# Differential attention on one Trainium2 core: two softmax maps of a head merged before the transpose instead of after the values product

## The chip, the core and the metric

The kernel runs on one core of one Trainium2 chip. The metric is the device time of one execution in microseconds. A core has five engines that run on their own and wait for each other by semaphores: TensorE (PE in the rows, with its weight loads as PEld), VectorE (DVE), ScalarE (ACT), GpSimd (POOL) and SyncE (SP, which here only starts the weight transfers). Each engine executes its own instructions strictly in the order in which the program gives them.

## What is computed

Two stacked models of two layers each act on 256 tokens of width 1024. The program has twelve stages: feed-forward, mixer, feed-forward, four times over. The change touches the last mixer alone, the stage `dil_diff` of the eleventh place, in which four heads of dilated attention and four heads of differential attention are computed. The differential part of the reference:

```python
def one_block(args):
    i, qa, qb = args
    ...
    s1 = jnp.where(causal, jnp.einsum('bqhd,bkhd->bhqk', qa, k1)..., -jnp.inf)
    s2 = jnp.where(causal, jnp.einsum('bqhd,bkhd->bhqk', qb, k2)..., -jnp.inf)
    attn = jax.nn.softmax(s1, axis=-1) - lam * jax.nn.softmax(s2, axis=-1)
    return jnp.einsum('bhqk,bkhe->bqhe', attn.astype(v.dtype), v)
```

So each head has two causal 256x256 maps. Their difference, with the weight `lam`, multiplies the head's values. After that each head's output is normalised, put beside the dilated heads and multiplied by the output weights.

## The kernel before

**Weights.** All weights come in pieces of 128x2048 floats through three slots. SP loads a piece, ACT copies it to a rounded high part `w_hi` (`split_hi`, line L460), DVE forms the low part `w_lo` as the difference (`split_lo`, L933), and PE multiplies with three matmuls per product (L1504 to L1506), 48 of 512 columns for a piece. ACT and DVE work two pieces ahead: at the start of their program for piece p both take piece p + 2 (`ahead`).

**The stage dil_diff** has 16 pieces. Pieces 0 to 11 project the tokens to dq, dk, dv, cq, ck and cv, two pieces for each; pieces 12 to 15 are the product with the output weights. A piece has two token tiles (tt 0 and 1). After each tile of the pieces 5 to 11, PE's program has a hook, `with_tile`, that does a little attention work between the big matmuls. It counts steps: step = 2 (p - 6) + tt + 1, so step 0 lies in piece 5, steps 1 and 2 in piece 6, 3 and 4 in piece 7 and so on. ACT and DVE have the same steps in their programs, behind the weight work of that piece.

**Maps.** The eight maps of the differential heads are numbered g0 to g0 + 7 (head h has maps 2h and 2h + 1), the four of the dilated heads follow. One map takes this route, and the maps follow each other one step apart:

- `scores` on PE (L1711), into bank 4 or 5;
- `soft` on DVE: scale and mask (L1371), then two maxima (L1374, L1375);
- `exp_map` on ACT: two exponentials with their sums (L572, four rows in the trace), in place;
- `turn_probs` on PE: three 128x128 transposes into bank 6 (L1719), two steps behind the scores;
- `take_probs` on ACT: bank 6 to SBUF (L580);
- `values` on PE: three fp32 matmuls into bank 7 (L1730, L1732, L1733), three steps behind the scores.

When both maps of head h are through `values`, DVE's `take_pair` (L1254 to L1261) inverts the sums, multiplies the second by -lam, and scales and adds the two 128x128 results of each token tile: six instructions. `square_head` on ACT (L811), `head_mean_square` on DVE (L1277), a power on POOL (L339) and `norm_head` on DVE (L1283) follow. The probabilities of a map lie in one of two buffers (map number modulo 2), so `soft` of map g waits for the transposes of map g - 2.

**On POOL,** `rotate_cq` runs four elementwise instructions on SBUF (L355, L356, L358, L360) as soon as ACT has taken cq in its program for piece 7.

**Order on the engines.** There is no scheduler; the order is written out. ACT's program for a piece of the map steps, which also takes the projected chunk in odd pieces (L564), is

```python
ahead(n0 + p)
for step in steps_of(p, 6, 1):
    if 2 <= step < 10:
        take_probs(g0 + step - 2)
    if step < 8:
        exp_map(g0 + step, step)
    if step in (5, 7, 9):
        square_head((step - 5) // 2)
```

and DVE's is `ahead`, then for each step `soft`, and in even steps from 4 `take_pair`. At piece 10 DVE also rotates ck (L1360 to L1363).

Of the kernel before, what the change touches and what calls it, by code (L numbers as in the profile page):

```python
# [71 lines left out]
def build(nc, program, t):  # L72
# [16 lines left out]
    with ExitStack() as ctx:  # L89
# [61 lines left out]
        merged_ready = sem("branches_merged")  # L151
        id_in = sem("ident_in")
# [107 lines left out]
        def psum3(b, k):  # L260
# [8 lines left out]
                       cqt=1024, ckt=1024, qa=1024, qb=1024, dkt=1024, diff=1024, sq=1024, prod=256,  # L269
# [18 lines left out]
        heads = lambda v, w=64: v.rearrange("p (t h d) -> p t h d", t=TT, d=w)  # L288

# [152 lines left out]
        def _(act):  # L442
# [124 lines left out]
            def exp_map(g, i):  # L567

                act.wait_ge(max_ready, g + 1)
                pr = A["probs"][:, (g % 2) * 384:(g % 2) * 384 + 384]  # L570
# [229 lines left out]
            def dil_diff(k):  # L800
# [13 lines left out]
                for p in range(PIECES["dil_diff"]):  # L814
                    ahead(n0 + p)
                    for step in steps_of(p, 6, 1):
                        if 2 <= step < 10:
                            take_probs(g0 + step - 2)
# [22 lines left out]
                    if p == 12:  # L841
                        take_probs(g0 + 8)
                        take_probs(g0 + 9)
                        exp_map(g0 + 10, 2)
                        exp_map(g0 + 11, 3)
                    if p == 13:
                        take_probs(g0 + 10)
                        take_probs(g0 + 11)
# [58 lines left out]
        def _(dve):  # L907
# [330 lines left out]
            def dil_diff(k):  # L1238
# [11 lines left out]
                def take_pair(h):  # L1250

                    dve.wait_ge(pv_done, g0 + 2 * h + 2)
                    i = 2 * h
                    link(nc.vector.reciprocal(expsum[:, 1, :, i:i + 2], expsum[:, 0, :, i:i + 2]))  # L1254
                    second = expsum[:, 1, :, i + 1]
                    link(nc.vector.tensor_scalar(second, second, lam[:, 5:6], None, ALU.mult))
                    for tt in range(TT):
                        prod = B["prod"][:, tt * P:(tt + 1) * P]
                        link(nc.vector.tensor_scalar(prod, bank[7][:, tt * 256 + P:tt * 256 + 256],
                                                     expsum[:, 1, tt, i + 1:i + 2], None, ALU.mult))  # L1260
                        ins = nc.vector.scalar_tensor_tensor(out=d4[:, tt, h], in0=bank[7][:, tt * 256:tt * 256 + P],  # L1261
                                                             scalar=expsum[:, 1, tt, i:i + 1], in1=prod, op0=ALU.mult, op1=ALU.add)
                    ins.then_inc(o_ready, 1)


# [23 lines left out]
                for p in range(last + 1):  # L1289
                    if p == 13:  # L1290
                        take_round(g0 + 9, 0, 2, x4[:, :, 0])
# [25 lines left out]
                    if p == 11:  # L1317
                        pair_low(bt0[k], 6, first_half)
                        pair_low(bt0[k] + 1, 7, second_half)
                        soft(g0 + 8, DIL_SCALE, B["mask_dil"])  # L1320
                        soft(g0 + 9, DIL_SCALE, B["mask_dil"])
                    if p == 12:
                        soft(g0 + 10, DIL_SCALE, B["mask_dil"])
                        soft(g0 + 11, DIL_SCALE, B["mask_dil"])
                    if p == 13:
                        pair_low(bt0[k] + 2, 4, beside)
                        take_round(g0 + 11, 2, 2, x4[:, :, 1])
# [37 lines left out]
            def soft(g, scale, mask):  # L1365

                pr = A["probs"][:, (g % 2) * 384:(g % 2) * 384 + 384]
                dve.wait_ge(s_done, g + 1)
                if g >= 2:
                    dve.wait_ge(pt_done, g - 1)  # L1370
                nc.vector.scalar_tensor_tensor(out=pr, in0=bank[4 + g % 2][:, 0:384], scalar=scale, in1=mask,  # L1371
# [129 lines left out]
        def _(pe):  # L1501
# [212 lines left out]
            def turn_probs(g):  # L1714
                pe.wait_ge(exp_done, g + 1)
                if g >= 1:
                    pe.wait_ge(pt_ready, g)
                for c in range(3):
                    ins = nc.tensor.transpose(bank[6][:, c * P:(c + 1) * P],  # L1719
                                              A["probs"][:, (g % 2) * 384 + c * P:(g % 2) * 384 + (c + 1) * P], ident[:, :])  # L1720
# [408 lines left out]
            def dil_diff(k):  # L2129
# [10 lines left out]
                def diff_values(m):  # L2140
                    values(g0 + m, m % 2, 2, [dv[:, tt, (m // 2) * P:(m // 2 + 1) * P] for tt in range(TT)], r0 + m // 2)
# [4 lines left out]
                def dil_values(m):  # L2146
                    values(g0 + 8 + m, m % 2, 2, [cv[:, tt, m * P:(m + 1) * P] for tt in range(TT)], r0 + 4 + m // 2)

                def with_tile(p, tt):
# [42 lines left out]
                def between(i, tt, h):  # L2192
                    slot = 4 * i + 2 * tt + h
                    if slot == 1:
                        turn_probs(g0 + 8)
                    if slot == 2:
                        turn_probs(g0 + 9)
# [6 lines left out]
                    if slot == 4:  # L2204
                        turn_probs(g0 + 10)
                        dil_values(1)
                    if slot == 5:
                        turn_probs(g0 + 11)
# [173 lines left out]
```

## Time and profile before

| | |
|---|---|
| median of 3 runs | 2100.21 us (2097.95 to 2101.26) |
| profiled execution | 2102.05 us, of it 2100.2 us span |
| mean granted TensorE clock | 0.996 |
| busy share of the span | PE 98%, PEld 82%, DVE 73%, ACT 49%, POOL 4% |
| chain that ended last | PE 90%, DVE 4%, ACT 3% |
| steps 0 to 10 of dil_diff | 1825.5 to 1869 us of the span |
| whole stage dil_diff | about 1795 to 1908 us |

The busy shares are means over twelve stages. Whether PE, or a loop through ACT and DVE, sets the pace in the 45 us that the change touches is read from the timelines and waits of that stretch alone. A matmul's duration in a row is longer than its share of PE's time, since matmuls overlap: PE's pace is read from the starts of the rows.

### The profile page before, as it was taken

The numbers are of one execution on the slowest core, as the hardware profiler recorded it, in microseconds if no ns is written. First come the engines' busy times: TensorE is split into PE (matmuls) and PEld (weight loads), VectorE is DVE, ScalarE is ACT, GpSimd is POOL, SyncE is SP. The second block draws the span as 40 slices with busy tenths as digits, with TensorE's granted clock in tenths as the row PEclk, the third lists the DMA queues.
The fourth block names the chain that finished last, engine by engine and source line by source line (L and its number), as shares of the span: only waits on it lengthen the run. The fifth ranks groups of instructions, "written<-read, shape, count | busy, mean of one in ns | idle before, by whom it ended". The sixth has DMA issues, their size and how long they took to land.

```text
span 2100.2 us, 26966 instructions
## 1 busy us (share of the span) xinstructions
PE 2062.7 (98%) x9770; PEld 1718.2 (82%) x9770; DVE 1537.7 (73%) x2408; ACT 1024.3 (49%) x1273; POOL 91.5 (4%) x98
## 2 busy tenths in 40 slices
PE   8999999999999999999999999999999999999998
PEld 6888887888788888788888879888888888778887
DVE  6787756878678776678777867557876887676876
ACT  5445554444544555444454457535445444655443
POOL 1000100000100010000010000210001000020000
PEclk9999999999999999999999999999999999999999
DMA  7554543555655453455555543315555555434552
GB/s 286 211 192 162 196 143 143 198 200 200 223 204 200 160 184 146 152 200 186 206 204 208 184 160 135 111 69 188 181 204 192 210 190 198 159 110 164 190 205 105
DMA packets 53955, 376.08 MB, mean 179 GB/s; under 512 B 6512, under 2 KB 6656, under 8 KB 9216
## 3 DMA queue, kind: packets, MB, share of 16 engines
q1 hardware_dynamic: 51120, 364.93, 47.5%
q0 software_dynamic: 2480, 10.16, 1.5%
q8 instruction: 46, 0.75, 0.1%
q14 instruction: 21, 0.17, 0.0%
q10 hardware_dynamic: 288, 0.07, 0.0%
HBM read 374.08 MB, written 1.05 MB: 179 GB/s over the span
## 4 chain that ended last, share of the span: by engine, by line
PE 90%; DVE 4%; ACT 3%; DMA 1%; issue 1%; POOL 0%; POOLq 0%; ACTq 0%; DVEq 0%; SPq 0%
PE bank L1504 28%; PE bank L1506 27%; PE bank L1505 27%; DVE w_lo L933 1%; DMA w_raw<-weights_dram 1%; ACT w_hi L460 1%; PE bank L1513 1%; PE bank L1711 1%; PE bank L1914 1%; PE bank L1925 1%; DVE mix L1076 0%; PE bank L1696 0%; PE bank L1924 0%; DVE mix L985 0%; PE bank L1872 0%
## 5 line engine op out<-in xcount | busy, mean ns | idle before, releaser
L933 DVE TENSOR_TENSOR w_lo<-w_raw,w_hi 128x2048 fp32r<-128x2048 f32 x344 | 786.7, 2291 | 265.3 <-ACT w_hi L460 169.0
L1504 PE MATMUL bank<-w_hi,xt_hi 128*128 128x512 f32 x1888 | 747.7, 396 | 10.9 <-DVE w_lo L933 7.0
L1506 PE MATMUL bank<-w_hi,xt_lo 128*128 128x512 f32 x1888 | 737.2, 390 | 0.0
L1505 PE MATMUL bank<-w_lo,xt_hi 128*128 128x512 f32 x1888 | 736.3, 390 | 0.0
L532 ACT ACTIVATE w_hi<-w_raw 128x2048 fp32r<-128x2048 f32 x192 | 366.5, 1910 | 131.2 <-PE bank L1506 131.2
L1504 PEld LDWEIGHTS bank<-w_hi,xt_hi 128*128 128x128 f32 x1888 | 355.5, 188 | 85.2 <-DVE w_lo L933 9.5
L1506 PEld LDWEIGHTS bank<-w_hi,xt_lo 128*128 128x128 f32 x1888 | 355.1, 188 | 75.3
L1505 PEld LDWEIGHTS bank<-w_lo,xt_hi 128*128 128x128 f32 x1888 | 355.6, 188 | 70.9
L985 DVE STREAM_TRANSPOSE mix<-hid 32x128 f32<-32x128 f32 x1152 | 349.0, 303 | 17.2
L460 ACT ACTIVATE w_hi<-w_raw 128x2048 fp32r<-128x2048 f32 x152 | 290.3, 1916 | 120.1 <-PE bank L1506 108.1
L1504 PE MATMUL bank<-w_hi,ht_hi 128*128 128x512 f32 x672 | 262.6, 391 | 1.2 <-issue 1.2
L1506 PE MATMUL bank<-w_hi,ht_lo 128*128 128x512 f32 x672 | 261.6, 389 | 0.0
L1505 PE MATMUL bank<-w_lo,ht_hi 128*128 128x512 f32 x672 | 261.5, 389 | 0.0
L501 ACT ACTIVATE gate<-bank,stat 128x256 f32<-128x256 f32 x176 | 83.3, 474 | 240.5 <-PE bank L1506 240.4
L511 ACT ACTIVATE ht_hi<-mix 128x512 fp32r<-128x512 f32 x72 | 45.6, 633 | 288.2 <-DVE mix L985 288.2
L975 DVE SCALAR_TENSOR_TENSOR hid<-bank,stat,gate 128x256 f32<-128x256 f32 x176 | 83.8, 480 | 101.2 <-ACT gate L501 101.0
L1504 PEld LDWEIGHTS bank<-w_hi,ht_hi 128*128 128x128 f32 x672 | 126.2, 188 | 27.8 <-issue 2.0
L1506 PEld LDWEIGHTS bank<-w_hi,ht_lo 128*128 128x128 f32 x672 | 126.1, 188 | 26.4
L1505 PEld LDWEIGHTS bank<-w_lo,ht_hi 128*128 128x128 f32 x672 | 126.2, 188 | 25.9
L331 POOL TENSOR_TENSOR stat<-stat,minus_half 128x1 f32<-128x1 f32 x26 | 14.3, 552 | 1749.0 <-DVE stat L938 1749.0
L487 ACT ACTIVATE xt_hi<-bank,gain 128x128 fp32r<-128x128 f32 x192 | 54.3, 371 | 51.8 <-PE bank L1513 49.1
L963 DVE SCALAR_TENSOR_TENSOR xt_lo<-bank,gain,xt_hi 128x128 fp32r<-128x128 f32 x192 | 53.6, 343 | 21.5 <-ACT xt_hi L487 19.5
(260 smaller groups left out, 1442.4 us busy)
## 6 DMA issues: line engine op xcount, KB each, us to landing
w_raw<-weights_dram SPq DMA_DIRECT2D x345, 1024.0 KB, 4.8
mix<-a_b_gate_dram POOLq DMA_DIRECT2D x4, 1024.0 KB, 14.7
mix<-a_pool_mean_dram POOLq DMA_DIRECT2D x2, 768.0 KB, 5.9
x<-x_dram SPq DMA_DIRECT2D x4, 256.0 KB, 7.4
w_raw<-weights_dram SPq DMA_DIRECT2D x4, 256.0 KB, 5.3
out_dram<-xn SPq DMA_DIRECT2D x2, 512.0 KB, 2.6
mix<-a_pool_w_dram POOLq DMA_DIRECT2D x2, 256.0 KB, 3.6
mix<-g_ret_dram POOLq DMA_DIRECT2D x1, 512.0 KB, 4.6
```

Source lines behind the costliest of these rows:

```text
L460: nc.scalar.activation(w_hi[s][:, :], w_raw[s][:, :], ACT.Copy).then_inc(hi_done, 1)
L487: ins = nc.scalar.activation(xt_hi[:, 4 * g + q, toks], psum3(4 + j, 4)[:, q, :], ACT.Copy, scale=gain[:, c:c + 1])
L501: nc.scalar.activation(gate[:, tt, :], b[:, 0:CH], ACT.Silu, scale=stat[:, 2, tt:tt + 1]).then_inc(gate_ready, 1)
L511: nc.scalar.activation(hidden_parts(c)[0], src.rearrange("p (k q) -> p k q", k=2), ACT.Copy).then_inc(ht_hi_done, 1)
L532: nc.scalar.activation(w_hi[s][:, :], w_raw[s][:, :], ACT.Copy).then_inc(hi_done, 1)
L933: nc.vector.tensor_tensor(w_lo[s][:, :], w_raw[s][:, :], w_hi[s][:, :].bitcast(F32), ALU.subtract).then_inc(lo_done, 1)
L963: ins = nc.vector.scalar_tensor_tensor(out=xt_lo[:, 4 * g + q, toks], in0=psum3(4 + j, 4)[:, q, :], scalar=gain[:, c:c + 1], in1=xt_hi[:, ...
L975: nc.vector.scalar_tensor_tensor(out=hid[:, tt, :], in0=b[:, CH:2 * CH], scalar=stat[:, 2, tt:tt + 1], in1=gate[:, tt, :], op0=ALU.mult, o ...
L985: ins = nc.vector.transpose(dst, src)
L1504: nc.tensor.matmul(out, a_hi, b_hi, start=start, stop=False)
L1505: nc.tensor.matmul(out, a_hi, b_lo, start=False, stop=False)
L1506: return nc.tensor.matmul(out, a_lo, b_hi, start=False, stop=stop)
```

## The change

DVE now merges the two probability maps of a head before the transposes, and everything behind works once per head. `merge_maps(h)` takes the place of `take_pair(h)`; it stands in DVE's even steps 2, 4, 6 and 8, ahead of the `soft` of that step, and waits for the exponentials of both maps. PE turns the merged map in steps 3, 5, 7 and 9 and multiplies with the values in steps 4, 6, 8 and 10; ACT's `take_probs` is called four times instead of eight; `take_head` on DVE is one copy from bank 7. The maps get four buffers of their own (`map_probs`), so `soft` of a differential map no longer waits for transposes. The dilated maps keep their method, with new numbers in the counting of transposes.

```diff
@@ DVE
-                def take_pair(h):
-                    dve.wait_ge(pv_done, g0 + 2 * h + 2)
+                def merge_maps(h):
                     i = 2 * h
+                    dve.wait_ge(exp_done, g0 + i + 2)
+                    if h >= 2:
+                        dve.wait_ge(pt_done, g0 + h - 1)
                     link(nc.vector.reciprocal(expsum[:, 1, :, i:i + 2], expsum[:, 0, :, i:i + 2]))
                     second = expsum[:, 1, :, i + 1]
                     link(nc.vector.tensor_scalar(second, second, lam[:, 5:6], None, ALU.mult))
+                    out = B["merged"][:, (h % 2) * 384:(h % 2) * 384 + 384]
+                    cols = (slice(0, P), slice(P, 3 * P))
                     for tt in range(TT):
-                        prod = B["prod"][:, tt * P:(tt + 1) * P]
-                        link(nc.vector.tensor_scalar(prod, bank[7][:, tt * 256 + P:tt * 256 + 256],
-                                                     expsum[:, 1, tt, i + 1:i + 2], None, ALU.mult))
-                        ins = nc.vector.scalar_tensor_tensor(out=d4[:, tt, h], in0=bank[7][:, tt * 256:tt * 256 + P],
-                                                             scalar=expsum[:, 1, tt, i:i + 1], in1=prod, op0=ALU.mult, op1=ALU.add)
-                    ins.then_inc(o_ready, 1)
+                        ins = nc.vector.tensor_scalar(out[:, cols[tt]], probs_of(g0 + i + 1)[:, cols[tt]],
+                                                      expsum[:, 1, tt, i + 1:i + 2], None, ALU.mult)
+                    link(ins)
+                    for tt in range(TT):
+                        ins = nc.vector.scalar_tensor_tensor(out=out[:, cols[tt]], in0=probs_of(g0 + i)[:, cols[tt]],
+                                                             scalar=expsum[:, 1, tt, i:i + 1], in1=out[:, cols[tt]],
+                                                             op0=ALU.mult, op1=ALU.add)
+                    ins.then_inc(maps_merged, 1)
+                def take_head(h):
+                    dve.wait_ge(pv_done, g0 + h + 1)
+                    nc.vector.tensor_copy(d4[:, :, h], bank[7]...[:, :, 0, :]).then_inc(o_ready, 1)
...
                     for step in steps_of(p, 6, 1):
+                        if step in (2, 4, 6, 8):
+                            merge_maps((step - 2) // 2)
                         if step < 8:
-                            soft(g0 + step, 0.125, B["mask"])
+                            soft(g0 + step, 0.125, B["mask"], 0)
                         if step in (4, 6, 8, 10):
-                            take_pair((step - 4) // 2)
+                            take_head((step - 4) // 2)
@@ ACT
-                        if 2 <= step < 10:
-                            take_probs(g0 + step - 2)
+                        if step in (3, 5, 7, 9):
+                            take_probs(g0 + (step - 3) // 2)
@@ PE
-                    if 2 <= step < 10:
-                        turn_probs(g0 + step - 2)
+                    if step in (3, 5, 7, 9):
+                        turn_merged_maps((step - 3) // 2)
                     if 0 <= step < 8:
                         diff_scores(step)
-                    if 3 <= step < 11:
-                        diff_values(step - 3)
+                    if step in (4, 6, 8, 10):
+                        diff_values((step - 4) // 2)
```

On DVE, in the program for piece 6 and the start of piece 7 (steps 1 to 3), before:

```order
L1371 SCALAR_TENSOR_TENSOR mix<-bank,mix 128x384 [waits probs_transposed,scores_done]
L1374 TENSOR_REDUCE negmax<-mix 128x1 [waits scores_masked]
L1375 TENSOR_REDUCE negmax<-mix 128x1
L1371 SCALAR_TENSOR_TENSOR mix<-bank,mix 128x384 [waits probs_transposed,scores_done]
L1374 TENSOR_REDUCE negmax<-mix 128x1 [waits scores_masked]
L1375 TENSOR_REDUCE negmax<-mix 128x1
L933 TENSOR_TENSOR w_lo<-w_raw,w_hi 128x2048 [waits hi_done]
```

and after, where L1393, L1396 and L1397 are the three lines of `soft` and L941 is `split_lo`:

```order
L1393 SCALAR_TENSOR_TENSOR mix<-bank,mix 128x384 [waits scores_done]
L1396 TENSOR_REDUCE negmax<-mix 128x1 [waits scores_masked]
L1397 TENSOR_REDUCE negmax<-mix 128x1
L1264 RECIPROCAL expsum<-expsum 128x2x2 [waits exp_done]
L1266 TENSOR_SCALAR expsum<-expsum,mix 128x2 [waits dve_step]
L1270 TENSOR_SCALAR mix<-mix,expsum 128x128 [waits dve_step]
L1270 TENSOR_SCALAR mix<-mix,expsum 128x256
L1274 SCALAR_TENSOR_TENSOR mix<-mix,expsum 128x128 [waits dve_step]
L1274 SCALAR_TENSOR_TENSOR mix<-mix,expsum 128x256
L1393 SCALAR_TENSOR_TENSOR mix<-bank,mix 128x384 [waits scores_done]
L1396 TENSOR_REDUCE negmax<-mix 128x1 [waits scores_masked]
L1397 TENSOR_REDUCE negmax<-mix 128x1
```

Between the two `soft` of a piece, which followed each other, there now stand six instructions, and the first of them waits for ACT.

On ACT, at the same place (exponentials of maps 1 and 2, then the high part of the next piece and map 3), before:

```order
L572 ACTIVATE mix,expsum<-mix,negmax 128x128 [waits max_ready]
L572 ACTIVATE mix,expsum<-mix,negmax 128x256
L580 ACTIVATE mix<-bank 128x384 [waits pv_done,probs_transposed]
L572 ACTIVATE mix,expsum<-mix,negmax 128x128 [waits max_ready]
L572 ACTIVATE mix,expsum<-mix,negmax 128x256
L460 ACTIVATE w_hi<-w_raw 128x2048 [waits piece_used,weights_landed0]
```

and after, where L580 is now the line of `exp_map`, L468 that of `split_hi` and L588 that of `take_probs`:

```order
L580 ACTIVATE mix,expsum<-mix,negmax 128x128 [waits max_ready]
L580 ACTIVATE mix,expsum<-mix,negmax 128x256
L580 ACTIVATE mix,expsum<-mix,negmax 128x128 [waits max_ready]
L580 ACTIVATE mix,expsum<-mix,negmax 128x256
L468 ACTIVATE w_hi<-w_raw 128x2048 [waits piece_used,weights_landed0]
L588 ACTIVATE mix<-bank 128x384 [waits pv_done,probs_transposed]
```

The copy of the transposes has left the place between the exponentials and stands once per piece behind the high part, which still comes after the second exponential.

## Rows read from the trace of the kernel before

**Rows 1.** Waits of 1800 to 1912 us: who waited for whom, total us, times, longest.
```profile
ACT mix L572 <- DVE negmax L1375: 23.2, 8, 4.5
DVE w_lo L933 <- ACT w_hi L460: 19.7, 9, 4.0
...
PE bank L1719 <- ACT mix L580: 2.5, 3, 1.4
...
PE bank L1711 <- ACT mix L867: 0.9, 1, 0.9
```

**Rows 2.** Timeline of PE: start us, duration us, instruction, idle before and releaser.
```profile
1828.85 0.81 PE L1711 MATMUL bank<-mix 128*128 128x128 f32 x4
...
1832.25 0.49 PE L1719 MATMUL bank<-ident,mix 128*128 128x128 f32 x3
...
1841.20 0.82 PE L1711 MATMUL bank<-mix 128*128 128x128 f32 x4
...
1845.62 0.82 PE L1711 MATMUL bank<-mix 128*128 128x128 f32 x4
...
1856.89 0.46 PE L1730 MATMUL bank<-mix 128*128 128x128 f32 x2 [1.62 <-DVE mix L1261]
```

**Rows 3.** Timeline of ACT, steps 1 and 2, with the high parts around them.
```profile
1829.57 1.90 ACT L460 ACTIVATE w_hi<-w_raw 128x2048 fp32r<-128x2048 f32 x1
1834.95 0.40 ACT L572 ACTIVATE mix<-mix,negmax 128x128 f32<-128x128 f32 x1 [3.47 <-DVE negmax L1375]
...
1835.84 0.47 ACT L580 ACTIVATE mix<-bank 128x384 f32<-128x384 f32 x1
1836.21 0.39 ACT L572 ACTIVATE mix<-mix,negmax 128x128 f32<-128x128 f32 x1
...
1837.09 1.90 ACT L460 ACTIVATE w_hi<-w_raw 128x2048 fp32r<-128x2048 f32 x1
```

**Rows 4.** Timeline of DVE, pieces 6 and 7.
```profile
1831.51 2.29 DVE L933 TENSOR_TENSOR w_lo<-w_raw,w_hi 128x2048 fp32r<-128x2048 f32 x1 [4.00 <-ACT w_hi L460]
1833.72 0.55 DVE L1371 SCALAR_TENSOR_TENSOR mix<-bank,mix 128x384 f32<-128x384 f32 x1
...
1843.46 0.17 DVE L1254 RECIPROCAL expsum<-expsum 128x4 f32<-128x4 f32 x1
...
1843.92 0.35 DVE L1259 TENSOR_SCALAR mix<-bank,expsum 128x128 f32<-128x128 f32 x1
```

**Rows 5.** One line of DVE: duration min/median/max ns, first and last start.
```profile
L1271 DVE TENSOR_SCALAR mix<-mix x1: 217/217/217, 1796.2 to 1796.2; 128x128 f32<-128x128 f32 x1
```

**Rows 6.** Groups of DVE of 1795 to 1912 us, by form: count, busy us, mean ns.
```profile
L1283 DVE SCALAR_TENSOR_TENSOR xn<-mix,hstat 128x128 f32<-128x128 f32 x8 | 2.4, 347 | 0.3 <-POOL hstat L339 0.3
```

**Rows 7.** Timeline of POOL: the last two instructions of rotate_cq.
```profile
1848.53 4.31 POOL L358 TENSOR_TENSOR mix<-mix 128x1024 f32<-128x1024 f32 x1
1852.92 2.38 POOL L360 TENSOR_TENSOR mix<-mix 128x1024 f32<-128x1024 f32 x1
```

**Rows 8.** Timeline of DVE, piece 8: soft of map 5, and the second instruction of take_pair(1).
```profile
1850.53 0.54 DVE L1371 SCALAR_TENSOR_TENSOR mix<-bank,mix 128x384 f32<-128x384 f32 x1
...
1852.95 2.38 DVE L1256 TENSOR_SCALAR expsum<-expsum,mix 128x2 f32<-128x2 f32 x1
```

**Rows 9.** Timeline of ACT: exponentials of maps 5 and 7, high parts of pieces 11 and 12.
```profile
1851.75 0.40 ACT L572 ACTIVATE mix<-mix,negmax 128x128 f32<-128x128 f32 x1 [3.72 <-DVE negmax L1375]
...
1854.48 1.90 ACT L460 ACTIVATE w_hi<-w_raw 128x2048 fp32r<-128x2048 f32 x1
...
1860.16 0.40 ACT L572 ACTIVATE mix<-mix,negmax 128x128 f32<-128x128 f32 x1 [3.41 <-DVE negmax L1375]
...
1863.15 1.91 ACT L460 ACTIVATE w_hi<-w_raw 128x2048 fp32r<-128x2048 f32 x1
```

**Rows 10.** Timeline of DVE, piece 10: start of take_pair(3) and the instruction behind it.
```profile
1872.07 0.17 DVE L1254 RECIPROCAL expsum<-expsum 128x4 f32<-128x4 f32 x1
...
1873.84 0.16 DVE L1277 TENSOR_SCALAR hstat<-hstat 128x2 f32<-128x2 f32 x1
```

More of the change, by code:

```diff
@@ L268, in build @@
         B = carve(dict(probs=768, probs_t=768, cq=1024, ck=1024, cv=1024, dq=1024, dk=1024, dv=1024, rot=1024, rot_q=1024,
-                       cqt=1024, ckt=1024, qa=1024, qb=1024, dkt=1024, diff=1024, sq=1024, prod=256,
+                       cqt=1024, ckt=1024, qa=1024, qb=1024, dkt=1024, diff=1024, sq=1024, prod=256, map_probs=1536, merged=768,
                        mask=384, mask_dil=384, rope=256, rope_wide=512, lambdas=256, diff_norm=128, lam=8))
@@ L288, in build, with probs_of @@
         heads = lambda v, w=64: v.rearrange("p (t h d) -> p t h d", t=TT, d=w)
+        def probs_of(g):
+            m = g - map0[program.index("dil_diff")]
+            if 0 <= m < 8:
+                return B["map_probs"][:, (m % 4) * 384:(m % 4) * 384 + 384]
+            return A["probs"][:, (g % 2) * 384:(g % 2) * 384 + 384]
         def causal_map(q_t, k_t, off, width):
@@ L841, in dil_diff @@
                     if p == 12:
-                        take_probs(g0 + 8)
-                        take_probs(g0 + 9)
+                        take_probs(g0 + 4)
+                        take_probs(g0 + 5)
                         exp_map(g0 + 10, 2)
@@ L1363, in rope, with soft @@
                 return nc.vector.tensor_tensor(x, x, rot, ALU.add)
-            def soft(g, scale, mask):
-                pr = A["probs"][:, (g % 2) * 384:(g % 2) * 384 + 384]
+            def soft(g, scale, mask, slot_free=None):
+                pr = probs_of(g)
                 dve.wait_ge(s_done, g + 1)
-                if g >= 2:
+                if slot_free is None and g >= 2:
                     dve.wait_ge(pt_done, g - 1)
+                if slot_free:
+                    dve.wait_ge(pt_done, slot_free)
                 nc.vector.scalar_tensor_tensor(out=pr, in0=bank[4 + g % 2][:, 0:384], scalar=scale, in1=mask,
@@ L1712, in scores, with turn_probs @@
                 ins.then_inc(s_done, 1)
[L1714 to L1717, printed above, removed]
+            def turn_probs(g, t=None, src=None):
+                if src is None:
+                    pe.wait_ge(exp_done, g + 1)
+                    src = probs_of(g)
+                t = g if t is None else t
+                if t >= 1:
+                    pe.wait_ge(pt_ready, t)
                 for c in range(3):
-                    ins = nc.tensor.transpose(bank[6][:, c * P:(c + 1) * P],
-                                              A["probs"][:, (g % 2) * 384 + c * P:(g % 2) * 384 + (c + 1) * P], ident[:, :])
+                    ins = nc.tensor.transpose(bank[6][:, c * P:(c + 1) * P], src[:, c * P:(c + 1) * P], ident[:, :])
                 ins.then_inc(pt_done, 1)
@@ L2138, in diff_scores, with turn_merged_maps, diff_values, turn_dil @@
                     scores(g0 + m, causal_map(mapped("qb" if m % 2 else "qa")[:, m // 2], mapped("dkt")[:, m // 2], 0, P))
-                def diff_values(m):
-                    values(g0 + m, m % 2, 2, [dv[:, tt, (m // 2) * P:(m // 2 + 1) * P] for tt in range(TT)], r0 + m // 2)
+                def turn_merged_maps(h):
+                    pe.wait_ge(maps_merged, h + 1)
+                    turn_probs(None, g0 + h, B["merged"][:, (h % 2) * 384:(h % 2) * 384 + 384])
+                def diff_values(h):
+                    values(g0 + h, 0, 2, [dv[:, tt, h * P:(h + 1) * P] for tt in range(TT)], r0 + h)
+                def turn_dil(m):
+                    turn_probs(g0 + 8 + m, g0 + 4 + m)
                 def dil_scores(m):
@@ L2146, in dil_values @@
                 def dil_values(m):
-                    values(g0 + 8 + m, m % 2, 2, [cv[:, tt, m * P:(m + 1) * P] for tt in range(TT)], r0 + 4 + m // 2)
+                    values(g0 + 4 + m, m % 2, 2, [cv[:, tt, m * P:(m + 1) * P] for tt in range(TT)], r0 + 4 + m // 2)
                 def with_tile(p, tt):
@@ L2194, in between @@
                     if slot == 1:
[L2195 removed]
+                        turn_dil(0)
                     if slot == 2:
[L2197 removed]
+                        turn_dil(1)
                         dil_scores(2)
```

24 lines of the change are left out of this document (13 added, 11 removed).

## The prediction

> **What bounds the kernel now.** I read the shares of the chain first, then the waits and the timelines of the 45 us that the change touches. Over the span PE is at work nearly all the time and makes up most of the chain. Inside the map steps PE's pace is read from the starts of its rows. The scores of two following tiles start at 1841.20 and 1845.62 [rows 2]: a tile with one turn, one scores, one values and twelve weight matmuls takes 4.42 us, a piece of two tiles 8.84 us. A tile with the scores alone takes 1832.25 - 1828.85 = 3.40 us [rows 2]. So PE pays 1.02 us for the turn and the values of one map.
>
> The second thing to see is how little room the other two engines have. In the waits [rows 1] ACT's exponentials wait 23.2 us for DVE's maxima and DVE's low parts wait 19.7 us for ACT's high parts. Two engines that wait for each other this much, while each also has the instruction that the other needs further down its own program, form a loop. Its order for one piece is: high part on ACT, low part on DVE, soft, exponential on ACT, the second exponential, next high part. The low part stands ahead of soft on DVE and both exponentials ahead of the next high part on ACT, so no round can overlap the next. A round lasts 1837.09 - 1829.57 = 7.52 us without a projected chunk [rows 3]. From the high part of piece 11 to that of piece 12 it is 1863.15 - 1854.48 = 8.67 us [rows 9]. The loop is thus only 0.2 us per piece faster than PE's 8.84 us: whatever is added to it beyond that comes out as time, however idle DVE looks as a share.
>
> **PE's and ACT's part of the change.** Four of eight turns and values go. On PE that frees 4 x 1.02 = 4.1 us. On ACT four copies L580 go, each 1836.21 - 1835.84 = 0.37 us [rows 3]. Both lie in the stretch at issue, but PE's gain only counts where PE sets the pace.
>
> **DVE's part: the instructions.** `merge_maps` starts as take_pair does: inversion and -lam together 1843.92 - 1843.46 = 0.46 us [rows 4]. Then come two tensor_scalars from SBUF, of 128 and 256 columns. The one such row has 128 columns and 0.217 us, with fixed factors [rows 5]; the two-column row of take_pair that reads its factor from SBUF cannot be much under that. The 128 more columns cost at most what a column costs in the low part, 2.29 us / 2048 = 1.1 ns [rows 4], that is 0.14 us. I take 0.28 and 0.35 us, bounds 0.22 to 0.35 and 0.28 to 0.49. Two scalar_tensor_tensors from SBUF follow: 0.35 us at 128 columns [rows 6], and 0.35 + 0.14 = 0.49 us at 256. Neighbours on DVE that don't wait overlap by some 0.08 us: the low part of 2.29 us is followed by soft after 1833.72 - 1831.51 = 2.21 us [rows 4]. Sum: 0.46 + 0.28 + 0.35 + 0.35 + 0.49 - 3 x 0.08 + 0.04 for the link = 1.73 us per head until the next instruction. The bounds are 1.55 and 1.95. `take_head`, one copy of 256 columns from a bank, is taken at 0.40 us; it has no row, and lies between the 0.35 us of a 128-column read of a bank [rows 4] and 0.35 + 0.14 us. take_pair took 1873.84 - 1872.07 = 1.77 us [rows 10]. By busy time DVE pays only 1.73 + 0.40 - 1.77 = 0.36 us more per head.
>
> **DVE's part: the wait.** The new wait is the main term. `merge_maps(h)` waits for the exponential of map 2h + 1, which DVE itself made possible one instruction earlier; behind the merge on DVE stands the soft of map 2h + 2, behind that the exponential of this map on ACT, and behind that ACT's next high part. Before, the two softs ran back to back and the two exponentials too. From the first exponential to the next high part ACT then took 1837.09 - 1834.95 = 2.14 us [rows 3]. After: the exponential until DVE may go on, 0.89 us (1835.84 - 1834.95) plus 0.14 us for its tail, as between ACT's high part and DVE's low part (1831.51 - 1829.57 = 1.94 us for a row of 1.90, and the accumulator read that still runs when ACT goes on) = 1.03; the merge 1.73; the soft until the exponential starts, 1834.95 - 1833.72 = 1.23 [rows 3, 4]; the exponential 0.88 (1837.09 - 1836.21). That is 4.87 us, so **+2.73 us per round**.
>
> - Piece 6 (head 0): +2.73. The high part of piece 9 starts at 1839.8 in place of 1837.09.
> - Piece 7 (head 1): the same, sum +5.46. The projected chunk on ACT behind it is unchanged.
> - Piece 8 (head 2): before, from the exponential of map 5 to the high part of piece 11, 1854.48 - 1851.75 = 2.73 us [rows 9], since the squares of head 0 lie there too. After, they hide under the merge: 4.87 - 2.73 = +2.14, sum +7.60.
> - Piece 8 again, **POOL**: rotate_cq starts when cq is taken, in every order the same time ahead of the low part of piece 10, so it moves along with the loop. The trace shows it and DVE shutting each other out. L358 took 4.31 us and L360, of the same size, 2.38 [rows 7]; the former got going only when DVE's low part was through. DVE's tensor_scalar L1256 of two columns started at 1852.95 and took 2.38 us [rows 8], just as long as L360, which had started at 1852.92. The soft at 1850.53, which reads a bank, ran beside L358 unharmed. Now count from the start of that soft: L358 ends at +2.31 (1848.53 + 4.31 - 1850.53) and L360 starts at +2.39. merge_maps(2) inverts at 1.23 + 1.03 = +2.26 and comes to its first tensor_scalar at +2.46. It again finds L360 at work and again loses 2.38 - 0.25 = 2.13 us. Before, this loss fell into DVE's wait for a high part but for some 0.3 us; now the soft of map 6 and the loop hang on it. Sum +9.73.
> - Piece 9 (head 3): before 8.67 us; after 1.94 + 2.21 + 1.23 = 5.38 to the exponential of map 7, then 2.99 (1863.15 - 1860.16) less the 0.37 of a copy that has moved ahead [rows 9] = 2.62; 8.00 us in all, -0.67. The last merge falls into DVE's wait for the high part. Sum +9.06.
> - Piece 10: DVE's low part, rotation of ck, norms and the end of head 3 follow one another. take_pair(3) becomes take_head(3): 0.40 - 1.77 = -1.37. Sum **+7.7 us**.
>
> **Why PE does not pay more, nor save.** PE waits for each merged map ahead of the turn, and the scores are queued behind it, but the next soft is always held by DVE's low part longer than that: merge 0 ends near 1837.7, the scores of map 3 are through near 1838.5, and DVE wants them at 1843.9. The values wait for ACT's copy behind a high part and still come 5 us or more before take_head asks. PE reaches the end of piece 11 about 0.2 us after the turned ck, where it used to wait 0.9 us for it [rows 1]. The dilated maps then have the same instructions in the same order, and nothing there is idle for long enough on both engines to win back the delay. All later stages start 7.7 us later.
>
> **A rule on the shared port.** The rows show that the loser waits for the whole instruction [rows 7, 8]. The Trainium skill (SBUF — State Buffer, Who interferes with whom) says so too, counts a VectorE instruction with two SBUF inputs among the contenders, and says that the one that starts first keeps the pair. What it would do if DVE came first is the second rival.
>
> **The sum.** The profiled execution takes 2102.05 us, 1.84 above the median of 2100.21. 2102.05 + 7.7 = 2109.8 for such an execution, 2100.21 + 7.7 = **2107.9 us** for the median. About 0.2%, 4.2 us, is what a measurement of this kernel tells from no change.
>
> **The rivals.**
>
> 1. *PE sets the pace, and the change does what it is meant to.* Then the 4.1 us of PE come off: 2096.1 us. For it: PE's share of the chain, and the single short wait of 1.62 us that DVE caused PE in the map steps [rows 2]. Against it: it decides at a loop of at most PE's new pace, 8.84 - 1.02 = 7.8 us for a piece, while the loop already takes 7.5 to 8.7 without the new wait. It would need the wait to be almost free. Chance 0.06.
> 2. *DVE gets ahead of L360.* The margin is 0.07 us (+2.46 against +2.39). If the merge takes the pair first and keeps it, 2.13 us fall out: +5.6, 2105.8 us. Against it: the merge has waits in it, where L360 would slip in. The named rule would give this time if DVE's start came first. Chance 0.15.
> 3. *The gaps behind the map steps take up part.* PE waited there 2.5 us for ACT's copies and 0.9 for ck [rows 1], less 0.3 inside the steps: 3.1 us. If these were slack, +7.7 - 3.1 = +4.6, 2104.8 us; with a merge at its lower bound less 3 x 0.18, 2104.3. Against it: they are waits of PE for the very engine that is late. Chance 0.09.
> 4. *More than one collision, or a merge at its upper bound.* 3 x 0.22 and a second shut-out by a late POOL instruction of 2.4 us: +10.8, 2111.0 us. Against it: rotate_cq has no further instruction behind L360. Chance 0.08.
>
> The forecast itself has 0.62, with a spread of its own from 2106 to 2109.5 (bounds of the merge, and 1.5 us of scatter in a median). The range 2103.5 to 2111.0 takes in the forecast and the rivals 2 and 3 and leaves out the first and the worst of the fourth. Faster by over 0.2% needs rival 1, which lies on that bound: 0.05. Within 0.2%: the rest of it, a part of rival 3 and the low tail of rival 2: 0.11. Slower: 0.84.
>
> **What the profile after would show.** DVE's inversion in merge_maps waits about 1.1 us for ACT, four times. The starts of the high parts of pieces 8 and 9 lie 10.2 us apart, the next 11.4, 13.0 and 8.0. PE waits for the merged map four times, 2 us or more each, near 5 us for head 2. One tensor_scalar of merge_maps(2) lasts some 2.4 us. After piece 12 every start lies 7 to 8 us later than now. Wrong would be: high parts at the old distance (the loop did not bind), or later stages that start where they did before.

## The result, and the profile after

The changed kernel takes 2107.9 us in the median of 6 runs (2105.16 to 2111.24), the kernel before, beside it, 2099.31 us (2096.41 to 2102.67). The ratio is 1.004 with a 95% interval of 1.003 to 1.0051: slower by 0.4%, 8.6 us by the medians.

The profiled execution of the changed kernel has a span of only 2103.4 us, 3.2 more than before. That is no contradiction. Whole executions scatter by several us, and the two that were profiled differed by about 4.4 us before they came to the stage. One line of DVE shows it, the sixteen gate additions of the first two mixers, the last of which lies in the second (count: duration min/median/max ns, first and last start; before, then after):

```profile
L1451 DVE SCALAR_TENSOR_TENSOR mix<-bank,stat,mix x16: 739/743/751, 261.3 to 832.9; 128x512 f32<-128x512 f32 x16
```

```profile
L1473 DVE SCALAR_TENSOR_TENSOR mix<-bank,stat,mix x16: 739/742/751, 260.1 to 828.4; 128x512 f32<-128x512 f32 x16
```

The change lies 1000 us behind 828. What it did is therefore read from a length that leaves out what comes before: from the start of ACT's high part of piece 8 (in the program for piece 6, ahead of the first merge) to the start of DVE's first addition to x behind the stage. Before it is 1906.71 - 1829.57 = 77.14 us, after 1909.84 - 1825.15 = 84.69 us: **+7.55 us**.

Timeline of ACT after (start, duration, instruction, idle before and releaser; L580 is the line of exp_map, L468 of split_hi), steps 1 and 2, to be set beside [rows 3], and the later high parts:

```profile
1825.15 1.90 ACT L468 ACTIVATE w_hi<-w_raw 128x2048 fp32r<-128x2048 f32 x1
1830.52 0.40 ACT L580 ACTIVATE mix<-mix,negmax 128x128 f32<-128x128 f32 x1 [3.48 <-DVE negmax L1397]
...
1834.50 0.40 ACT L580 ACTIVATE mix<-mix,negmax 128x128 f32<-128x128 f32 x1 [2.99 <-DVE negmax L1397]
...
1835.39 1.90 ACT L468 ACTIVATE w_hi<-w_raw 128x2048 fp32r<-128x2048 f32 x1
...
1846.78 1.91 ACT L468 ACTIVATE w_hi<-w_raw 128x2048 fp32r<-128x2048 f32 x1
...
1859.70 1.89 ACT L468 ACTIVATE w_hi<-w_raw 128x2048 fp32r<-128x2048 f32 x1
...
1867.69 1.91 ACT L468 ACTIVATE w_hi<-w_raw 128x2048 fp32r<-128x2048 f32 x1
```

The second exponential, which followed the first at once but for a copy, now has 2.99 us of idle time ahead of it, and the high part of piece 9 hangs behind it. On DVE the other half of the same wait (L1393 is soft's first line, L1264 to L1274 are merge_maps):

```profile
1829.29 0.55 DVE L1393 SCALAR_TENSOR_TENSOR mix<-bank,mix 128x384 f32<-128x384 f32 x1
...
1831.54 0.18 DVE L1264 RECIPROCAL expsum<-expsum 128x4 f32<-128x4 f32 x1 [1.05 <-ACT mix L580]
1831.76 0.23 DVE L1266 TENSOR_SCALAR expsum<-expsum,mix 128x2 f32<-128x2 f32 x1
1832.02 0.55 DVE L1270 TENSOR_SCALAR mix<-mix,expsum 128x128 f32<-128x128 f32 x2
1832.61 0.75 DVE L1274 SCALAR_TENSOR_TENSOR mix<-mix,expsum 128x128 f32<-128x128 f32 x2
1833.27 0.55 DVE L1393 SCALAR_TENSOR_TENSOR mix<-bank,mix 128x384 f32<-128x384 f32 x1
```

1.05 us of wait, 1833.27 - 1831.54 = 1.73 us of merge, then the next soft. PE's waits for the merged maps and for the copy (timeline of PE after, L1745 the transposes, L1755 the values):

```profile
1833.41 0.55 PE L1745 MATMUL bank<-ident,mix 128*128 128x128 f32 x3 [2.03 <-DVE mix L1274]
...
1843.65 0.55 PE L1745 MATMUL bank<-ident,mix 128*128 128x128 f32 x3 [2.20 <-DVE mix L1274]
...
1849.11 0.49 PE L1755 MATMUL bank<-mix 128*128 128x128 f32 x2 [0.83 <-ACT mix L588]
...
1857.72 0.90 PE L1745 MATMUL bank<-ident,mix 128*128 128x128 f32 x3 [4.90 <-DVE mix L1274]
```

And the meeting with POOL in piece 8, first DVE, then POOL (L366 and L368 are the last two instructions of rotate_cq), to be set beside [rows 7, 8]:

```profile
1851.54 0.55 DVE L1393 SCALAR_TENSOR_TENSOR mix<-bank,mix 128x384 f32<-128x384 f32 x1
...
1853.79 0.18 DVE L1264 RECIPROCAL expsum<-expsum 128x4 f32<-128x4 f32 x1 [1.05 <-ACT mix L580]
1854.00 2.30 DVE L1266 TENSOR_SCALAR expsum<-expsum,mix 128x2 f32<-128x2 f32 x1
```

```profile
1849.55 4.30 POOL L366 TENSOR_TENSOR mix<-mix 128x1024 f32<-128x1024 f32 x1
1853.93 2.34 POOL L368 TENSOR_TENSOR mix<-mix 128x1024 f32<-128x1024 f32 x1
```

DVE's two-column instruction came 0.07 us after L368 and ended with it.

### The profile page after: what moved, and what is told of

The parts are those of the page before. It is cut to its first block, busy times and chain, and to the rows that moved or that the text cites. A ratio compares the mean times of both kernels' runs of the same rounds, so it can differ in the third digit from the quotient of the medians.

```text
span 2103.4 us, 26878 instructions
## 1 busy us (share of the span) xinstructions
PE 2059.9 (98%) x9734; PEld 1715.1 (82%) x9734; DVE 1539.2 (73%) x2412; ACT 1023.1 (49%) x1269; POOL 89.5 (4%) x98
## 3 DMA queue, kind: packets, MB, share of 16 engines
HBM read 374.08 MB, written 1.05 MB: 178 GB/s over the span
## 4 chain that ended last, share of the span: by engine, by line
PE 90%; DVE 4%; ACT 3%; DMA 1%; issue 1%; POOL 0%; POOLq 0%; ACTq 0%; DVEq 0%; SPq 0%
PE bank L1526 28%; PE bank L1528 27%; PE bank L1527 27%; DVE w_lo L941 2%; ACT w_hi L468 1%; DMA w_raw<-weights_dram 1%; PE bank L1535 1%; PE bank L1733 1%; PE bank L1939 1%; PE bank L1950 1%; DVE mix L1084 0%; PE bank L1718 0%; PE bank L1949 0%; DVE mix L993 0%; PE bank L1897 0%
## 5 line engine op out<-in xcount | busy, mean ns | idle before, releaser
L941 DVE TENSOR_TENSOR w_lo<-w_raw,w_hi 128x2048 fp32r<-128x2048 f32 x344 | 786.8, 2291 | 266.3 <-ACT w_hi L468 170.0
L468 ACT ACTIVATE w_hi<-w_raw 128x2048 fp32r<-128x2048 f32 x152 | 290.4, 1916 | 118.2 <-PE bank L1528 108.3
```

What stands on the lines that cost most here:

```text
L468: nc.scalar.activation(w_hi[s][:, :], w_raw[s][:, :], ACT.Copy).then_inc(hi_done, 1)
L941: nc.vector.tensor_tensor(w_lo[s][:, :], w_raw[s][:, :], w_hi[s][:, :].bitcast(F32), ALU.subtract).then_inc(lo_done, 1)
```

## The experiments

Six kernels ran besides the changed one. Two readings stand for each: the time against the kernel before of the same chip, and the length of the stage in the profiled execution, as defined above, which isn't touched by the scatter ahead of the stage.

| kernel | time, us | kernel before beside it, us | ratio (95%) | stage, us | against before |
|---|---|---|---|---|---|
| before | | | | 77.14 | |
| changed kernel | 2107.9 | 2099.31 | 1.004 (1.003 to 1.0051) | 84.69 | +7.55 |
| e1_soft_first | 2099.87 | 2100.52 | 0.9996 (0.9987 to 1.0005) | 76.20 | -0.94 |
| e2_rotation_later | 2104.7 | 2100.52 | 1.0024 (1.0014 to 1.0034) | 82.61 | +5.47 |
| e3_wait_alone | 2101.27 | 2100.52 | 1.0004 (0.9995 to 1.0013) | 79.29 | +2.15 |
| e4_turn_later | 2103.85 | 2100.52 | 1.0016 (1.0007 to 1.0025) | 78.28 | +1.14 |
| e5_both_orders | 2098.55 | 2099.67 | 0.9993 (0.9984 to 1.0002) | 74.76 | -2.38 |
| e6_scaled_twice | 2109.76 | 2099.67 | 1.0053 (1.0039 to 1.0066) | 86.48 | +9.34 |

Distances of the starts of ACT's high parts, from that of piece 8 to that of piece 12, in us. They are the rounds of the loop. The last column is the rest of the stage, from the high part of piece 12 to the first addition to x:

| kernel | 8 to 9 | 9 to 10 | 10 to 11 | 11 to 12 | rest |
|---|---|---|---|---|---|
| before | 7.52 | 8.65 | 8.74 | 8.67 | 43.56 |
| changed kernel | 10.24 | 11.39 | 12.92 | 7.99 | 42.15 |
| e1_soft_first | 7.38 | 8.90 | 8.37 | 8.96 | 42.59 |
| e2_rotation_later | 10.25 | 11.37 | 10.85 | 8.00 | 42.14 |
| e3_wait_alone | 8.53 | 9.66 | 9.17 | 8.36 | 43.57 |
| e4_turn_later | 7.38 | 8.52 | 8.94 | 8.00 | 45.44 |
| e5_both_orders | 7.39 | 8.87 | 8.38 | 7.99 | 42.13 |
| e6_scaled_twice | 10.84 | 11.98 | 13.53 | 7.99 | 42.14 |

The rest is the same to 0.02 us in the changed kernel, e2, e5 and e6, and in the kernel before and e3. Within each of these two groups the rounds alone make the difference. One profile stands behind each row; how well such lengths repeat shows in this column and in rounds that an edit doesn't touch (10.24 and 10.25, 11.39 and 11.37). In e1 and e4 PE adds to the rest, as shown below.

### The place of the wait

Theory: the merge costs what it does since it stands, with its wait, between the two softs of a piece. Rival: the merge's own instructions, and PE's waits for its result, are the cost wherever it stands.

```diff
+                        if step < 8:
+                            if step >= 2:
+                                dve.wait_ge(exp_done, g0 + step - 1)
+                            soft(g0 + step, 0.125, B["mask"], 0)
                         if step in (2, 4, 6, 8):
                             merge_maps((step - 2) // 2)
-                        if step < 8:
-                            soft(g0 + step, 0.125, B["mask"], 0)
```

> The changed kernel with one thing undone: in DVE's even steps soft of the next map stands ahead of merge_maps, so that DVE waits for the exponential of map 2h+1 with that soft already behind it (soft gets a wait of its own for an exponential two maps back, long past). Theory of the loop: the way from the exponential of map 2h+1 to ACT's next high part falls from 4.87 us to about 2.1 to 2.4, all of the four distances of high parts (pieces 8 to 12) come down from 10.2, 11.4, 12.9, 8.0 to about 7.4, 8.7, 8.6, 8.3, and the time falls by 6.5 to 9 us against the changed kernel, to 0 to 2.5 us under the kernel before. PE still waits for merges 0 and 2, about 2 and 3 to 5 us. Rival (the merge's own instructions and PE's wait for them are the cost, not the place of the wait): the same instructions run, so the time stays within 2 us of the changed kernel, 6 or more over the kernel before.

The same instructions in this order give back everything: the stage falls by 84.69 - 76.20 = 8.49 us, the time to that of the kernel before within its interval. DVE, same place as above (L1395 soft, L1264 the first of merge_maps):

```profile
1829.26 0.55 DVE L1395 SCALAR_TENSOR_TENSOR mix<-bank,mix 128x384 f32<-128x384 f32 x1
...
1830.38 0.55 DVE L1395 SCALAR_TENSOR_TENSOR mix<-bank,mix 128x384 f32<-128x384 f32 x1
...
1831.51 0.18 DVE L1264 RECIPROCAL expsum<-expsum 128x4 f32<-128x4 f32 x1
```

The inversion starts at the same distance from the first soft, 2.25 us, as in the changed kernel. The 1.05 us in which DVE had nothing to do are now filled by the second soft, and ACT gets on. The rival's first half falls: with the same instructions the cost is gone. Its second half, PE's waits, is not excluded by this run, since they shrink too: PE waits 2.03 us for the first merge and 3.15 for the third, where it waited 2.03, 2.20 and 4.90. It falls by the changed kernel's own trace, where from the first merge to the high part of piece 12 no idle time of ACT or DVE ends with PE, and by the last column of the table.

The last round was forecast at 8.3 us and is 8.96, since here merge_maps(2) is held up by POOL, and DVE begins the low part of piece 11 about 1 us after ACT's high part is ready. PE gets the merged map late for the same reason. DVE, then PE (L1747 is the turn):

```profile
1848.64 2.35 DVE L1266 TENSOR_SCALAR expsum<-expsum,mix 128x2 f32<-128x2 f32 x1
```

```profile
1852.41 0.81 PE L1747 MATMUL bank<-ident,mix 128*128 128x128 f32 x3 [3.15 <-DVE mix L1274]
```

From this row PE works without a wait until 1880.42. At the end of the map steps PE is now the late one: ACT waits 0.33 us for it and DVE 0.64 for ACT behind that, where DVE waits 0.21 in e5. That makes up the 0.44 us by which the rest of the stage is longer than in the changed kernel.

### The wait without the merge

The kernel before, with nothing but the wait:

```diff
                     for step in steps_of(p, 6, 1):
+                        if step in (2, 4, 6, 8):
+                            dve.wait_ge(exp_done, g0 + step)
                         if step < 8:
                             soft(g0 + step, 0.125, B["mask"])
```

> The kernel before with nothing but a wait on DVE: ahead of the even softs (maps 2, 4, 6) and in step 8 it waits for the exponential of the map before, where merge_maps waits in the changed kernel. No instruction is added. Theory of the loop: ACT's way from one exponential to the next high part grows from 2.14 to 1.03 + 1.23 + 0.88 = 3.14 us in the pieces 6 and 7 (+1.0 each) and from 2.73 to 3.14 in piece 8 (+0.4), and 0.3 is won back from POOL's collision: +2.1 us in the high part of piece 12 and at the end, against the kernel before. Rival (PE sets the pace and the loop has slack): the stage's end is unmoved, 0 +- 0.5 us.

```profile
DVE mix L1373 <- ACT mix L572: 3.2, 3, 1.1
```

DVE waits three times 1.06 us (waits of DVE in e3_wait_alone, 1820 to 1870 us), the rounds grow by 1.01, 1.01 and 0.43 us, the last one shrinks by 0.31, and the stage grows by 2.15 us where 2.1 was expected. The first two waits come out almost whole, though DVE idles 27% of the span. Of the third only 0.43 us does, since ACT had the squares of head 0 to do in that place before. The time itself, 0.75 us over before with an interval of -0.05% to +0.13%, can't tell 2 us from nothing; the stage can.

### POOL's part

```diff
                 pool.wait_ge(cq_steps, 2)
+                pool.wait_ge(maps_merged, 3)
                 nc.gpsimd.tensor_tensor(q, q, rot, ALU.add).then_inc(cq_ready, 1)
```

> The changed kernel with POOL's last instruction of rotate_cq held until the third merge is done, so that it can't meet merge_maps(2). Theory (the collision costs what the instruction is held up): the second instruction of merge_maps(2) lasts 0.23 us in place of 2.30, the high part of piece 11 comes 2.1 us earlier after that of piece 10 (10.8 in place of 12.9 us), and the time is 2.1 us under that of the changed kernel, about 5.5 to 6.5 over the kernel before. PE's longest wait falls from 4.9 us to about 2.8. Rival (the collision is hidden as it was before the change, or another instruction meets POOL instead): the time of the changed kernel within 0.7 us, 7.5 or more over the kernel before.

DVE and POOL of this kernel in piece 8 (L1267 is merge_maps' second instruction, L1296 head_mean_square, L369 the instruction that waits):

```profile
1854.17 0.23 DVE L1267 TENSOR_SCALAR expsum<-expsum,mix 128x2 f32<-128x2 f32 x1
...
1857.12 1.19 DVE L1296 TENSOR_SCALAR hstat<-hstat 128x2 f32<-128x2 f32 x1
```

```profile
1855.91 2.38 POOL L369 TENSOR_TENSOR mix<-mix 128x1024 f32<-128x1024 f32 x1 [1.88 <-DVE mix L1275]
```

The stage is 84.69 - 82.61 = 2.08 us shorter, all of it in the round from piece 10 to 11 (12.92 to 10.85). The time goes from 8.6 to 4.2 us over before, more than 2.1 us and to less than the 5.5 to 6.5 that were expected, but the two comparisons have intervals that overlap. POOL's instruction did meet another one of DVE, head_mean_square, which takes 1.19 us in place of 0.16; behind it DVE waits 1.42 us for ACT anyway, so it costs nothing. What each of the two collisions cost was set by what stood behind the loser.

### One to one

```diff
-                    for tt in range(TT):
-                        ins = nc.vector.tensor_scalar(out[:, cols[tt]], probs_of(g0 + i + 1)[:, cols[tt]], ...)
-                    link(ins)
+                    for again in range(2):
+                        for tt in range(TT):
+                            ins = nc.vector.tensor_scalar(out[:, cols[tt]], probs_of(g0 + i + 1)[:, cols[tt]], ...)
+                        link(ins)
```

> The changed kernel with the two tensor_scalars of merge_maps and their link executed twice (the same result is written again). They take 0.59 us per head on DVE. Theory (the merge stands in a loop without slack, but for head 3, whose merge falls into a wait of 1.3 us): the high part of piece 12 and the end of the stage come 3 x 0.59 = 1.8 us later than in the changed kernel, 86.5 us from the high part of piece 8 to the first addition to x in place of 84.7. Rival (DVE's idle time of some 2 to 4 us per piece takes it up): 84.7 us, no change.

The three first rounds grow by 0.60, 0.59 and 0.61 us, the fourth by nothing; the stage by 86.48 - 84.69 = 1.79 us. The added instructions count whole in the first three merges, and not at all in the last one, which falls into a wait of DVE for ACT.

### Two tries at a faster order

If PE's waits for merges 0 and 2 mattered once soft is first, turning a step later should win:

```diff
-                    if step in (3, 5, 7, 9):
+                    if step in (4, 6, 8, 9):
                         turn_merged_maps((step - 3) // 2)
...
-                    if step in (4, 6, 8, 10):
+                    if step in (5, 7, 9, 10):
                         diff_values((step - 4) // 2)
```

on top of e1's order, with take_head in DVE's steps 5, 7, 9 and 10, and squares and means behind it.

> As e1_soft_first, and PE turns the merged maps of heads 0 to 2 one step later (steps 4, 6, 8, and 9 for head 3) and takes the values a step later too; take_head, squares and means follow. Theory: PE's waits for merges 0 and 1 vanish and that for merge 2 falls below 2 us, but the loop of ACT and DVE sets the end: the high part of piece 12 comes where it does in e1 within 0.5 us, and the time is that of e1 or up to 1.5 us less, 1 to 3 us under the kernel before. Rival (PE's waits set the end once soft is first): 2 us or more faster than e1.

Theory and rival both missed. The high part of piece 12 comes 32.84 us after that of piece 8, in e1 33.61, so the loop is even a little quicker (0.77 us, half a us was allowed); but the stage is 2.08 us longer than in e1, and the time 4 us. I had forgotten what take_head(2) is now queued behind. DVE and PE in piece 10 (L1385 ends the rotation of ck, L1282 is take_head, L1295 head_mean_square; on PE L1757 the values of head 3, L1720 the turns of cq):

```profile
1867.87 1.23 DVE L1385 TENSOR_TENSOR mix<-mix 128x1024 f32<-128x1024 f32 x1
1869.02 0.42 DVE L1282 COPY mix<-bank 128x256 f32<-128x256 f32 x1
...
1873.09 0.17 DVE L1295 TENSOR_SCALAR hstat<-hstat 128x2 f32<-128x2 f32 x1 [1.71 <-ACT mix L819]
```

```profile
1869.58 0.46 PE L1757 MATMUL bank<-mix 128*128 128x128 f32 x2 [1.42 <-DVE mix L1282]
...
1870.32 1.04 PE L1720 MATMUL bank<-ident,mix 128*128 128x128 f32 x8
```

take_head(2) stands behind DVE's low part and the rotation of ck; bank 7 is free only then, so PE's values of head 3 wait, cq is turned late, ACT copies it late, and the squares of head 3 stand behind that copy: DVE waits 1.71 us for them where it waited 0.69. From the high part of piece 12 to that of 13 it is 11.80 us, against 9.97 in e1. The next distance is 10.35 us against 9.31: from 1869.58 PE works without a wait until 1885.71 and is the late one, ACT waits 1.10 us for it, and DVE in turn for ACT:

```profile
1879.45 0.69 DVE L1413 TENSOR_TENSOR bt_lo<-bank,bt_hi 128x512 fp32r<-128x512 f32 x1 [1.66 <-ACT bt_hi L592]
```

So a queue on DVE cost the first 1.83 us, and PE, made late by it, the next 1.04; the loop gave 0.77 back.

The other try keeps e1 and takes POOL's last instruction to a place where DVE reads a bank:

```diff
                 pool.wait_ge(cq_steps, 2)
+                pool.wait_ge(lo_done, first_piece[k] + 12)
```

> As e1_soft_first, and POOL's last instruction of rotate_cq waits until DVE has split piece 11, so that it runs beside the soft of map 7, which reads a bank. Theory: merge_maps(2) is no longer held up, DVE splits piece 11 about 1 us earlier (8.0 in place of 8.96 us between the high parts of pieces 11 and 12), and the stage from the high part of piece 8 to the first addition to x is about 74.8 us, against 76.2 in e1 and 77.1 in the kernel before: about 2 us (0.1%) under the kernel before. Rival (PE's waits for the merges, not the loop, set the end in e1, or the instruction collides elsewhere): 76.2 us or more for the stage, no gain on e1.

The stage is 74.76 us, the last round 7.99. This is the shortest stage of all, 2.38 us under the kernel before and 9.9 under the changed one. Of the 1.44 us under e1, 0.97 come in the last round, as expected. The other 0.46 come in the rest of the stage, where PE, which waits 1.06 us for the third merge in place of 3.15, is no longer late; the expectation had the number but did not name this part. The time, 2098.55 against 2099.67 us, ratio 0.9993 (0.9984 to 1.0002), doesn't stand clear of no change; 2.4 us in 2100 is hardly more than the 0.09% on either side of that ratio. It beats the changed kernel; that it beats the one before is shown by the stage, not by the time.

## Why the prediction held, point by point

- **The bound.** That ACT and DVE form a loop without room for more was the step on which all else hung. e3 and e6 show it: what lengthens a round, by a bare wait or by two more instructions, lengthens the stage by as much (2.14 and 2.15 us, 1.80 and 1.79). The reason given for it was weaker than the result. The 0.2 us of room compare the last round, 8.67 us, with PE's 8.84. By the same comparison the first round, 7.52 us, had 1.3 us of room, yet in e3 1.01 us in it came out whole. What decides is who is late where the two meet, and at the end of the map steps PE waited for ACT's copy of ck already, 0.88 us before the change and 0.89 in e3. The sum took nothing off for room, and was right in that.
- **The merge.** Forecast 1.73 us, 1.73 measured. The pair of scalings measured 0.59 us to the next start (forecast 0.59), the inversion and -lam 1832.02 - 1831.54 = 0.48 (0.46), take_head 1859.03 - 1858.69 = 0.34 to the next start (0.40), just under its lower bound of 0.35:

```profile
1858.69 0.42 DVE L1282 COPY mix<-bank 128x256 f32<-128x256 f32 x1
1859.03 0.16 DVE L1295 TENSOR_SCALAR hstat<-hstat 128x2 f32<-128x2 f32 x1
```

- **The wait.** Forecast 1.03 from the exponential until DVE goes on; 1831.54 - 1830.52 = 1.02. Per round +2.73 forecast; 10.24 - 7.52 = +2.72 and 11.39 - 8.65 = +2.74.
- **POOL.** Counted from the start of soft, DVE was forecast at +2.46 and L360's counterpart at +2.39; they came at 1854.00 - 1851.54 = 2.46 and 1853.93 - 1851.54 = 2.39. The loss is 2.30 - 0.23 = 2.07 us (forecast 2.13). The round gave 12.92 - 8.74 = +4.18 (forecast 2.14 + 2.13 = 4.27).
- **The end.** Rounds together +8.96 (forecast +9.06), take_pair to take_head 0.34 - 1.77 = -1.43 (forecast -1.37): +7.53, and 7.55 at the end of the stage (forecast 7.7). The rest of the stage behind piece 12 shrank by 43.56 - 42.15 = 1.41. By the medians it is 8.6 us, with an interval of 6 to 11 us.
- **PE.** Forecast: four waits for the merged maps of 2 us or more. There were three; the fourth merge found PE still at work, since PE's clock had fallen (below). From the third turn to the fourth PE took 1867.96 - 1857.72 = 10.24 us. In e2, where the clock had not fallen there, PE was through 7.99 us after the third turn and waited 2.25. That the values would always come long before they were asked for was right for take_head, but PE itself waited 0.83 us for a copy; neither reached the end. PE's rows have twelve weight matmuls for a tile, as the prediction counts them, and so 24 for a piece; the 48 in the description of the weights is too many.
- **The rivals.** The first (PE sets the pace) falls with e3; the second (DVE ahead of L360) did not happen by 0.07 us of order, and was not run: e2, where the two instructions don't meet, shows +5.5 and makes its +5.6 plausible, no more; the third falls since the gaps of PE for ACT's copies are still there, with 1.46 and 0.82 us, and the one for ck gave way to a gap of 1.18 us a tile earlier; of the fourth nothing was seen. DVE's low part of piece 10 did lose to POOL as well, 2.90 in place of 2.29 us, but it took 2.92 in the kernel before.

The median of 2107.9 us equals the forecast to a tenth. That is chance: single executions scatter by 6 us, the kernel before measured 2099.31 us where the forecast had started from 2100.21, and the stage alone says 7.55, not 8.6.

## What to carry to other kernels

An engine with much idle time can still have none to give: where two in-order engines wait for each other inside a round, lay out the round instruction by instruction, and look which of the three engines is late where they meet; a comparison of mean paces alone would have shown room here that was not there. A new instruction that waits for the other engine belongs behind everything that the other engine needs next; here the same six instructions with their wait cost 8.5 us of the stage or nothing, by their place before or behind one soft. Where whole executions scatter more than the effect, measure the length of the stage between two fixed instructions of the trace.

## What the runs showed of the hardware

PE's clock was not expected to play a part. Stretches of the changed kernel (us: PE, PEld, DVE, ACT, POOL busy with counts, granted clock, DMA):

```profile
1852.00:1856.00 4.00, 0.82 (x4) 0.35 (x2) 2.88 (x5) 1.57 (x8) 3.92 (x2) 1.00 0.73 262
1856.00:1860.00 4.00, 2.28 (x8) 2.10 (x9) 3.08 (x10) 1.19 (x5) 0.98 (x2) 0.60 0.00 0
1860.00:1864.00 4.00, 4.00 (x11) 3.09 (x11) 2.37 (x2) 1.97 (x2) 0.00 (x0) 0.54 0.00 0
1864.00:1868.00 4.00, 3.92 (x21) 2.99 (x20) 2.80 (x10) 2.93 (x11) 0.00 (x0) 1.00 0.69 236
```

After the 4.90 us without a matmul the granted clock is at about 0.54 to 0.60, that is mostly at the lower of its two levels, 1.2 GHz, and the starts of weight matmuls lie 0.43 us apart:

```profile
1861.83 0.63 PE L1528 MATMUL bank<-w_hi,xt_lo 128*128 128x512 f32 x1
1862.26 0.63 PE L1526 MATMUL bank<-w_hi,xt_hi 128*128 128x512 f32 x1
...
1865.43 0.39 PE L1528 MATMUL bank<-w_hi,xt_lo 128*128 128x512 f32 x1
1865.66 0.40 PE L1526 MATMUL bank<-w_hi,xt_hi 128*128 128x512 f32 x1
```

From 1863.8 on they lie 0.23 apart again. In the changed kernel it cost nothing: in e2_rotation_later, whose longest wait of PE is 2.83 us, the clock stayed at 1.00 in these stretches, and the stage was shorter by just the collision. PE, which waits for the merges, had time to lose.

How long PE had waited does not by itself tell whether the clock falls. The wait of 2.03 us ahead of the first merged turn left it at 1.00 in the changed kernel and in e1_soft_first. In e2, with the same program up to there, it fell:

```profile
1833.59 0.68 PE L1746 MATMUL bank<-ident,mix 128*128 128x128 f32 x3 [2.03 <-DVE mix L1275]
```

```profile
1834.00:1836.00 2.00, 2.00 (x8) 1.71 (x7) 0.61 (x3) 1.31 (x5) 0.00 (x0) 0.50 0.00 0
```

After 2.83 us in e2 it stayed, after 2.85 us in e4_turn_later it fell, to 0.57 in the 4 us from 1860. The first rounds of e2 are still those of the changed kernel, 10.25 and 11.37 us against 10.24 and 11.39, so this fall cost nothing either.

It isn't free everywhere. After the 3.15 us of wait in e1 the clock fell to 0.64 and 0.75 in the stretches behind it. From the third merged turn to the values behind it PE took 1857.86 - 1852.41 = 5.45 us, and for the same work at 1.00 in e5_both_orders 1857.42 - 1853.63 = 3.79. These 1.66 us are part of what makes PE late in e1, where the stage's rest is 0.44 us longer. How much of the 0.44 they are was not separated from the longer wait.

The other thing is how small an instruction can be that is shut out by POOL: two columns of a tensor_scalar from SBUF, 2.30 us in place of 0.23, and in e2 a statistic of two columns, 1.19 in place of 0.16. The statistic reads one operand from SBUF and has fixed factors, so it takes no second input to be shut out. It came while POOL's instruction ran and ended 0.02 us after it (1857.12 + 1.19 against 1855.91 + 2.38). The rule of the Trainium skill (SBUF — State Buffer, Who interferes with whom), that the later of the two waits for the whole instruction of the other, holds in each of these rows.
